# A decoder step on one core: a head's small products gathered into three breaks of a round, pages loaded to match, and the sums of squares moved from TensorE to GpSimd

## The reference

```
h = rms_norm(x);  u = h @ w_in                       # 2048 x 11264
hq, hf, hi, hgate, dq, dk, dv, g_hg, g_da = split(u)
o_hg = hgrn2(hq, hf, hi)                             # 8 heads, chunks of 64 tokens, own state per sample
o_hg = rms_norm(o_hg per head) * silu(hgate)
o_da = diff_attend(dq, dk, dv, bias)                 # two softmax maps per head; samples over 2048 paged keys
o_da = rms_norm(o_da per head) * (1 - lam_init)
mixed = (sigmoid(g_hg) * (o_hg @ w_hg) + sigmoid(g_da) * (o_da @ w_da)) @ w_out
x = x + rms_norm(mixed)
x = x + rms_norm((silu(gate) * up) @ w_down)
```

## Time and profile before

| | |
|---|---|
| median of three runs | 1895.16 us (1894.0 to 1895.21) |
| the profiled execution | 1895.32 us, span 1893.7 us |
| TensorE, VectorE, ScalarE, GpSimd busy | 99%, 55%, 44%, 4% |
| granted TensorE clock | 0.999 of full speed |
| DMA engines' busy share in a round | 0.93 to 0.94 |
| one round | 78.7 us |

### The profile page before, as it was taken

The page is one execution under the profiler, slowest core; times in us unless marked ns, Lnnn a source line. Parts: engine busy times, 40 slices in busy tenths (PEclk is TensorE's granted clock), DMA queues, the critical chain, the costliest instruction groups (busy, mean ns, idle before and its releaser), DMA issues.

```text
span 1893.7 us, 38262 instructions
## 1 busy us (share of the span) xinstructions
PE 1883.7 (99%) x14742; PEld 1778.2 (94%) x14742; DVE 1050.4 (55%) x1401; ACT 826.3 (44%) x1083; POOL 74.7 (4%) x119
## 2 busy tenths in 40 slices
PE   9999999999999999999999999999999999999998
PEld 9999888888888888899999999999999999999998
DVE  8443655656556565665647754445444445455555
ACT  6333454435544355454445433333333334445454
POOL 1001010000100000000000000000000000000000
PEclk9999999999999999999999999999999999999999
DMA  8877899999999899977544544454544454444541
GB/s 318 178 259 257 325 352 343 376 341 350 350 345 376 335 354 354 345 276 275 178 155 148 168 163 158 142 176 166 162 159 155 155 176 156 157 165 151 171 155 56
DMA packets 123998, 444.27 MB, mean 235 GB/s; under 512 B 14581, under 2 KB 18693, under 8 KB 123872
## 3 DMA queue, kind: packets, MB, share of 16 engines
q1 hardware_dynamic: 112720, 402.31, 59.2%
q0 software_dynamic: 9984, 39.63, 7.3%
q10 hardware_dynamic: 1232, 1.47, 0.2%
HBM read 423.43 MB, written 22.54 MB: 236 GB/s over the span
## 4 chain that ended last, share of the span: by engine, by line
PE 97%; DMA 1%; DVE 1%; ACT 0%; issue 0%; SPq 0%; DVEq 0%
PE ps L449 50%; PE ps L438 6%; PE ps L439 6%; PE ps L440 6%; PE ps L1869 5%; PE ps L1870 5%; PE ps L1871 5%; PE ps L959 3%; PE ps L994 3%; PE ps L1511 3%; PE ps L968 1%; DMA raw<-w_hg 1%; DMA gates<-uT 0%; PE ps L780 0%; DVE ffn L1831 0%; PE ps L719 0%
## 5 line engine op out<-in xcount | busy, mean ns | idle before, releaser
L374 DVE TENSOR_TENSOR w_lo<-raw,w_hi 128x1024 fp32r<-128x1024 f32 x416 | 503.4, 1223 | 480.4 <-ACT w_hi L369 243.7
L369 ACT ACTIVATE w_hi<-raw 128x1024 fp32r<-128x1024 f32 x236 | 246.5, 1057 | 367.6 <-PE ps L449 302.2
L1869 PE MATMUL ps<-hid_hi,w_hi 128*128 128x320 f32 x680 | 203.4, 299 | 0.0
L1870 PE MATMUL ps<-hid_hi,w_lo 128*128 128x320 f32 x680 | 203.3, 299 | 0.0
L1871 PE MATMUL ps<-hid_lo,w_hi 128*128 128x320 f32 x680 | 203.3, 299 | 0.0
L449 PE MATMUL ps<-x_hi,w_hi 128*128 128x320 f32 x1200 | 191.4, 303 | 0.2 <-ACT w_hi L381 0.2
L449 PEld LDWEIGHTS ps<-x_hi,w_hi 128*128 128x128 f32 x1200 | 169.0, 189 | 21.7 <-issue 21.5
L397 ACT ACTIVATE w_hi<-raw 128x1024 fp32r<-128x1024 f32 x124 | 129.8, 1053 | 111.2 <-DMA raw<-w_in 96.4
L449 PE MATMUL ps<-x_hi,w_lo 128*128 128x320 f32 x1136 | 177.5, 299 | 0.0
L449 PE MATMUL ps<-x_lo,w_hi 128*128 128x320 f32 x1072 | 167.5, 299 | 0.0
L449 PEld LDWEIGHTS ps<-x_hi,w_lo 128*128 128x128 f32 x1136 | 161.9, 189 | 0.0
(11 more groups left out here) (366 smaller groups left out, 3073.5 us busy)
## 6 DMA issues: line engine op xcount, KB each, us to landing
raw<-w_in SPq DMA_DIRECT2D x176, 512.0 KB, 7.6
raw<-w_up SPq DMA_DIRECT2D x176, 512.0 KB, 3.5
raw<-ck SPq DMA_DIRECT2D x128, 512.0 KB, 5.9
raw<-cv SPq DMA_DIRECT2D x128, 512.0 KB, 6.4
raw<-w_dn SPq DMA_DIRECT2D x88, 512.0 KB, 3.5
raw<-w_out SPq DMA_DIRECT2D x32, 512.0 KB, 4.0
uT<-stage POOLq DMA_DIRECT2D x14, 640.0 KB, 4.1
raw<-w_hg SPq DMA_DIRECT2D x16, 512.0 KB, 4.8
```

Source lines behind the costliest of these rows:

```text
L369: act.activation(w_hi[slot % HALVES][:, :], raw[slot][:, :], ACT.Copy).then_inc(hi_ready, 1)
L374: dve.tensor_tensor(w_lo[half][:, :], raw[slot][:, :], w_hi[half][:, :].bitcast(F32), ALU.subtract).then_inc(lo_ready, 1)
L1869: pe.matmul(ps[:, m, 0:T], wh[:, c], xh, **dict(add, start=q == 0))
L1870: pe.matmul(ps[:, m, 0:T], wl[:, c], xh, **add)
```

## The change

TensorE's small products are in three breaks, behind A1, A4 and A6 (`ds_s` stays behind A7):

- behind A1: `new_scores`, `scores` and `vk`, key pages 0 to 3, `i_t`
- behind A4: `kd_t`, `a`, key pages 4 to 7, `ds`, `o_s0`
- behind A6: `pd_t`, key pages 8 to 11, `pv`, `o`

`pe_behind` is what comes behind the pages in a break. The loads are issued in an order that has three, then two, then one A granule between the groups of key pages, with the buffers as before. VectorE makes `w_lo` of A2 ahead of `vec_head(1)`, ScalarE's copy `pdt` is behind `w_hi` of A7. `sq_hi`, `sq_lo`, `norm_sums` and the matrix `ones_r` are gone: GpSimd does one `partition_all_reduce` of 128 x 576 into `sq_all`, behind the `v_new` DMA in its order, and the roots read `sq_all`.

```diff
-PLACES = {item: i % RING for i, item in enumerate(ROUND)}
-ROUND_SLOTS = dict(PLACES)
+PLACES = {item: i % RING for i, item in enumerate(BY_SLOT)}
+ROUND = (items("A", 0, 2) + items("K", 0, 4) + items("A", 2, 5) + items("K", 4, 8) + items("A", 5, 7)
+         + items("K", 8, 12) + items("A", 7, 8) + items("K", 12, 16) + items("D", 0, 4) + items("V", 0, 8)
+         + items("D", 4, 7) + items("V", 8, 16) + items("D", 7, 8))
+ROUND_SLOTS = {item: PLACES[item] for item in ROUND}
...
             if q == 6:
                 act.wait_ge(h_pe.sem, h_pe.at(h, "o_s0"))
                 h_act.done(act.activation(i_tok[:, 2, :], ps[:, 6, 2 * P:3 * P], ACT.Copy), "i_smp")
+            if q == 7:
                 act.wait_ge(h_pe.sem, h_pe.at(h, "pd_t"))
...
-                act.wait_ge(k_act.sem, k_act.at(r, "sq"))
-                k_act.done(act.activation(sq_hi[:, :], n_sq[:, :], ACT.Copy), "sh")
             elif what == "rt":
-                act.wait_ge(k_pe.sem, k_pe.at(r, "ss"))
+                act.wait_ge(k_pool.sem, k_pool.at(r, "ss"))
...
             for q in range(1, 8):
-                round_lo(dve, r, "A", q)
+                if q != 2:
+                    round_lo(dve, r, "A", q)
                 if q == 1:
                     vec_pages(dve, r, "new")
+                    round_lo(dve, r, "A", 2)
                 vec_head(dve, q, r)
...
                 in_products(pe, 8 * FIRST + 16 * r + q, q, lambda m: pe.wait_ge(set_out, 4 * gate_set(r) + m - 3))
+                if q == 1:
+                    new_scores(pe, r)
                 pe_head(pe, q, r)
-                if q == 0:
-                    new_scores(pe, r)
-                if q in (1, 3, 5):
-                    scores(pe, r, q // 2)
+                if q in (1, 4, 6):
+                    scores(pe, r, q // 3)
+                pe_behind(pe, q, r)
...
-            norm_sums(pe, r)
...
                 bass.ds(r, 1)].rearrange("a q d -> (a q) d")).then_inc(v_n_landed, 16)
+            k_pool.begin()
+            pool.wait_ge(k_act.sem, k_act.at(r, "sq"))
+            pool.sem_inc(passed, 1)
+            k_pool.done(pool.partition_all_reduce(sq_all[:, :], n_sq[:, :], channels=P, reduce_op=bass.bass_isa.ReduceOp.add), "ss")
             pool.wait_ge(head_stored, HEAD_STORES * (r + 1))
             pool.sem_inc(h_pool.sem, 1)
```

More of the change, by code:

```diff
@@ L238, in build @@
         n_rs, n_rs2 = n_sq[:, 0:T], n_sq[:, T:]
-        sq_hi = sb("sq_hi", [P, T + SEQ], F32R, at_mix)
-        sq_lo = sb("sq_lo", [P, T + SEQ], F32R, at_mix)
+        sq_all = sb("sq_all", [P, T + SEQ], F32, at_mix)
         at_mix.close()
@@ L313, in build @@
         v_n_landed = sem("v_n_landed")
-        k_pe = Steps(sem("k_pe"), "new s0 s1 s2 s3 ss", 1)
-        k_act = Steps(sem("k_act"), "q silu g0 g1 g2 g3 p sq sh rt rt_da", 1)
-        k_vec = Steps(sem("k_vec"), "new silu m0 m1 m2 near m3 mx nmx r w sl rs on og rs_da da", 1)
+        k_pe = Steps(sem("k_pe"), "new s0 s1 s2 s3", 1)
+        k_pool = Steps(sem("k_pool"), "ss", 1)
+        k_act = Steps(sem("k_act"), "q silu g0 g1 g2 g3 p sq rt rt_da", 1)
+        k_vec = Steps(sem("k_vec"), "new silu m0 m1 m2 near m3 mx nmx r w rs on og rs_da da", 1)
         v_pe = Steps(sem("v_pe"), "pt pn new ot", 1)
@@ L708, in vec_head, with to_tokens @@
                 h_vec.done(new_state(1, 5), "s_new")
+        def to_tokens(pe, src, samples, bank):
+            pe.sem_inc(passed, 1)
+            for j, tokens in enumerate((src[:, 0:P], src[:, P:SEQ], samples.rearrange("p j s t -> p (j s t)"))):
+                ins = pe.transpose(ps[:, bank, j * P:(j + 1) * P], tokens, ident[:, :])
+            return ins
         def pe_head(pe, q, h):
@@ L733, in pe_head @@
                 h_pe.done(ins, "vk")
[L734 to L739, removed]
+            if q == 4:
                 pe.wait_ge(h_vec.sem, h_vec.at(h, "qkd"))
-                h_pe.done(to_tokens(kd, kd_smp[:, :, :, :], 4), "kd_t")
+                h_pe.done(to_tokens(pe, kd, kd_smp[:, :, :, :], 4), "kd_t")
                 for c in (0, 2):
@@ L746, in pe_head, with pe_behind @@
                 h_pe.done(pe.matmul(ps[:, 5, SEQ:T], kg[:, KG_SMP:KG_SMP + P], qg[:, SEQ:T], start=True, stop=True), "a")
+            if q == 6:
+                pe.wait_ge(h_vec.sem, h_vec.at(h, "aT"))
+                for j in range(3):
+                    ins = pe.transpose(ps[:, 5, j * P:(j + 1) * P], pd[:, j * P:(j + 1) * P], ident[:, :])
+                h_pe.done(ins, "pd_t")
+            if q == 7:
+                pe.wait_ge(h_act.sem, h_act.at(h, "o_att"))
+                pe.wait_ge(h_vec.sem, h_vec.at(h, "own"))
+                for b in range(2):
+                    t = slice(CHUNK * b, CHUNK * b + CHUNK)
+                    ins = pe.matmul(ps[:, 6 - b, :], kd_tok[t, 2, :], i_own[t, :, :], start=True, stop=True)
+                h_pe.done(ins, "ds_s")
+        def pe_behind(pe, q, h):
+            x = stage[0]
+            if q == 1:
+                pe.wait_ge(set_out, 4 * hg_set(h) + 3)
+                pe.wait_ge(h_vec.sem, h_vec.at(h, "i_smp"))
+                pe.wait_ge(h_act.sem, h_act.at(h, "tok"))
+                h_pe.done(to_tokens(pe, x[:, 2, :], i_smp[:, :, :, :], 6), "i_t")
             if q == 4:
@@ L774, in pe_head @@
                 h_pe.done(pe.matmul(ps[:, 4, SEQ:T], i_tok[:, 2, :], aT[:, SEQ:T], start=True, stop=True), "o")
[L775 to L781, removed]
         def store_set(pool, s, at, tile):
@@ L916, in vec_pages @@
                 k_vec.done(dve.tensor_tensor(w_row[:, :], l_all[:, 1:2], cf[:, :], ALU.mult), "w")
-            elif what == "low_squares":
-                dve.wait_ge(k_act.sem, k_act.at(r, "sh"))
-                k_vec.done(dve.tensor_tensor(sq_lo[:, :], n_sq[:, :], sq_hi[:, :].bitcast(F32), ALU.subtract), "sl")
             elif what == "norm":
@@ L974, in turn_new @@
             v_pe.done(pe.transpose(ps[0:NQ, 7, 0:P], s_all[:, PAST:], ident[:, :]), "pn")
[L976 to L981, removed]
         def values(pe, r, g):
@@ L2122, in _ @@
             pool.sem_inc(h_pool.sem, 1)
+            pool.sem_inc(k_pool.sem, 1)
             pool.sem_inc(stage_free, 2)
```

14 lines of the change are left out of this document (4 added, 10 removed).

## The result

The changed kernel takes 1909.54 us (median of five runs, 1906.46 to 1915.12), the kernel before 1895.16 (1894.0 to 1895.29, five runs): ratio 1.0076, 95% interval 1.0066 to 1.0087. It is slower by 14.4 us where I had forecast no change, and lies above my range. The profiled execution took 1909.46 us, span 1907.8.

What follows compares the result with a forecast made beforehand. TensorE, busy 99% of the span, was taken as the bound. Rounds 0 to 6 add 0.08 us each (+0.6), the last round +1.9, together +2.5 on 1895.16: 1897.6 us, chance 0.42, range 1888.5 to 1907.

Steps and rivals of the forecast that it cites:

- the sentence on the loads: Key pages 12 to 15 wait for the second score group, about 4 us later, wanted at A7's end; costed at nothing.
- my rivals: ScalarE in time for A4 (0.22); all-reduce 7.6 to 20 us (0.27) or over 20 (0.05); reordering pays and costs nothing.
- something else: Any outcome outside the forecast and the rivals given chances; no place or size; chance 0.04.
- My own sign for it: List of what would show the forecast wrong, including a DMA transfer as releaser of a wait in any round.
- A4's wait, 1.0 us: Before A4's first product TensorE waits 1.0 us for ScalarE's `w_hi`, in every round.
- Breaks, 0.39 us a round: In the A half, fewer tile shape changes on TensorE save 0.39 us a round, bounds 0.2 and 0.6.
- Sums off TensorE, 0.53: Sums of squares leaving TensorE gain 0.53 us a round, bounds 0.5 and 0.64; GpSimd's all-reduce taken as 6 us.
- Last round, +1.3 at the turn: In the last round, softmax and the turn of the probabilities, for which TensorE already waited, come 1.3 us later.
- the fourth branch granule: In the last round TensorE waits 2.0 us here with a 6 us all-reduce; 0.5 left after the `o_rows` wait absorbs part.
- the forecast's own terms: Rounds 0 to 6, each: breaks -0.39, A4's wait +1.0, sums -0.53, together +0.08 us.

## Why the prediction was wrong, step by step

- **The step that failed** is the sentence on the loads: "Key pages 12 to 15 wait for the second group of scores, now about 4 us later, but are wanted at the end of A7 ... I cost these at nothing." The pages themselves were in time. They were issued 3.2 us later, not 4. I asked only when the delayed load is wanted, not what the DMA engines, at 0.93 of their time in a round, have to make up behind it; and I did not name the third group's release in ordinary rounds at all, though I had worked it out for the last one. The lateness arrives sixteen loads further on, at D4, which is issued 0.8 us later and lands 3.9 us later, in ScalarE's order ahead of a copy that TensorE needs. It cost 1.56 us in each of seven rounds, 10.9 us in all, most of the error. Shown by moving the copy (-12.8 us, 10.9 of them in the rounds, with D4 landing 2.0 to 5.1 us behind the turn's start), and by moving each group by itself. None of my rivals held this; it falls under "something else", to which I had given 0.04.
- **My own sign for it** was "if any round has a DMA as releaser". In the chain of waits of the changed kernel (start, length, what) that transfer is on the path once in each of rounds 0 to 6, as here in rounds 0 and 1:

```profile
237.04 12.79 DMA raw<-w_in
...
318.92 10.71 DMA raw<-w_in
```

- **A4's wait, 1.0 us: right place, size 0.62, and 0.72 with what it costs the granule behind it.** The exponential starts 6.35 us behind `new_scores`, not 6.58, and TensorE reaches A4 10.25 us behind it, not 10.13. From the exponential to the end of that `w_hi` it is 4.47 us, the number of the prediction.
- **Breaks, 0.39 us a round: 0.19 to 0.20**, the lower bound. One break more costs 0.05 (78.06 against 78.01). The single changes of shape, summed up from the rows, gave twice what gathering the breaks is worth; where the other half went is not shown.
- **Sums off TensorE, 0.53: 0.53.** The all-reduce takes 3.55 us where I had chosen 6, and no run waits for it in an ordinary round.
- **Last round, +1.3 at the turn: +1.6.** At the fourth branch granule the wait is 0.5 us, not 2.0, since the all-reduce is shorter; but the gates' wait, which I did not follow, grew by 1.6. The clock fell behind the turn's wait and no longer behind the one for `o_rows`; I had counted neither, and that they cancel is luck.
- With the measured sizes of the forecast's own terms a round is 78.73 - 0.53 - 0.19 + 0.72 = 78.73, no different from before, and the run with the copy moved shows 78.73. The mechanism that I forecast is real, and what lay over it was missing from the rivals.

## What to carry to other kernels

When work that releases a ring buffer moves, follow the queue from that load on to the first load that an in-order engine waits for, and see what stands behind that wait there. The loads on the way need not be issued late: with the DMA engines at 0.93 of their time, loads issued 3 to 4 us late left a load 10 to 16 places further on, itself issued less than 1 us late, to land 4 to 5 us late. Two releases can cross the room together where taking back either one all but ends the wait. A conversion that waits for a transfer should not stand ahead of a copy that another engine waits for, unless the transfer's room is larger than any delay of it. And if a wait seems to cost more than its own length, look at the granted clock behind it.

## What the runs showed of the hardware

- `partition_all_reduce` (add) of 128 x 576 float32 on GpSimd: 3.55 us, three in a row 3.55, 3.60, 3.59 with 0.2 us between them.
- The granted clock fell to the lower of its two levels, 1.2 GHz, behind some waits of TensorE and not behind others as long or longer. In the kernel before it fell in the last round, behind the wait of 1.46 us for `o_rows`; with both groups later it did not fall in round 0, behind 3.21 us. With the third group moved it fell in rounds 0, 2 and 3, after waits of 2.54, 2.01 and 2.75 us, and not in rounds 1 and 4, after 2.21 and 2.23; the value pages behind it took 5.35 us where 3.66 is usual. In round 0 of that run (busy time of TensorE, granted clock, DMA share, GB/s):

```profile
252.00:257.00 5.00, 4.76 (x57) 0.66 0.58 197
257.00:262.00 5.00, 5.00 (x47) 1.00 0.97 354
```

It cost 1.5 to 1.65 us each time. Of the run's 25 us the waits at the new probabilities are 15.5, the clock in the rounds 4.7, the last round 3.4. In rounds 0 to 6 of the changed kernel, with waits up to 2.30 us, it did not fall; in its last round it did, behind 2.5 us. What decides between a wait that has this price and one that has not stays open.
